# Four value tiles' products cut at 512 and 8, or at 348 and 172, token columns in place of 260 and 260

## The reference

```python
def rmsnorm(x, g):
    y = xf * lax.rsqrt(jnp.mean(xf * xf, axis=-1, keepdims=True) + EPS)
    return (y * g).astype(x.dtype)

def ab_mixer(h, conv_buf, past, w_in, b_f, conv_w, w_out):     # h = rmsnorm(x, g)
    q, k, v, f_lin, b_gate, c_gate, x_in = jnp.split(h @ w_in, AB_SPLITS, axis=-1)
    ...
    logf = jax.nn.log_sigmoid(f_lin + b_f)
    y_a = fox_prompt(q, k, v, logf)            # or fox_decode(...) for the sample tokens
```

## Time and profile before

| what | value |
|---|---|
| time, median of 3 runs | 2090.14 us (2089.59 to 2093.53) |
| the profiled execution's span | 2089.9 us |
| PE busy, share of the span | 2068.6 us, 99% |
| DVE busy | 1125.9 us, 54% |
| ACT busy | 702.9 us, 34% |
| value tiles v0 to v3 on PE | 445.3 to 472.0 us of the span |
| the time of the profiled execution by itself | not given apart; its span lies within the runs' times |

### The profile page before, as it was taken

How to read it: one execution, slowest core, us unless ns; L and a number is a source line. 1 busy time by engine, 2 the same in 40 slices (tenths; PEclk the granted TensorE clock), 3 DMA queues, 4 the chain that set the end, 5 groups by cost and what they waited for, 6 DMA issues and landing times.

```text
span 2089.9 us, 37944 instructions
## 1 busy us (share of the span) xinstructions
PE 2068.6 (99%) x17092; PEld 2046.3 (98%) x17092; DVE 1125.9 (54%) x1509; ACT 702.9 (34%) x877; POOL 47.7 (2%) x95
## 2 busy tenths in 40 slices
PE   8999999999999999999999999999999999999999
PEld 8999999999999999999999999999998999999998
DVE  6443244866768543244686342344898854323467
ACT  5221123423354322122444222122487432212243
POOL 0000000022200000000000000000000000000000
PEclk9999999999999999999999999999999999999999
DMA  5222222145321322222222222222222222222222
GB/s 175 90 90 89 96 102 81 62 153 162 127 108 61 122 81 92 91 102 92 101 82 101 82 96 89 99 84 79 86 97 84 82 101 102 89 94 85 98 92 82
DMA packets 35106, 202.79 MB, mean 97 GB/s; under 512 B 5088, under 2 KB 5376, under 8 KB 17024
## 3 DMA queue, kind: packets, MB, share of 16 engines
q1 hardware_dynamic: 29520, 183.87, 25.0%
q0 software_dynamic: 5424, 16.50, 2.5%
HBM read 193.78 MB, written 4.48 MB: 95 GB/s over the span
## 4 chain that ended last, share of the span: by engine, by line
PE 86%; DVE 11%; ACT 2%; issue 1%; DMA 1%; DVEq 0%; ACTq 0%
PE acc L1825 70%; PE acc L1935 10%; DVE w_lo L1120 2%; DVE t L1233 2%; PE acc L1866 1%; DVE x L1240 1%; DVE act_lo L1246 1%; DMA raw<-in_weights 1%; DVE rs_post L1228 1%; PE acc L2015 1%; PE acc L2069 1%; DVE xsum L1255 1%; DVE rs_pre L1228 0%; PE acc L2093 0%; PE acc L2142 0%
## 5 line engine op out<-in xcount | busy, mean ns | idle before, releaser
L1825 PE MATMUL acc<-act_hi,w_hi 128*128 128x260 f32 x3072 | 621.5, 284 | 0.0
L1825 PE MATMUL acc<-act_hi,w_lo 128*128 128x260 f32 x3072 | 617.8, 283 | 0.0
L1825 PE MATMUL acc<-act_lo,w_hi 128*128 128x260 f32 x3072 | 617.4, 282 | 0.0
L1825 PEld LDWEIGHTS acc<-act_hi,w_hi 128*128 128x128 f32 x3072 | 472.4, 188 | 2.7 <-issue 2.0
L1825 PEld LDWEIGHTS acc<-act_hi,w_lo 128*128 128x128 f32 x3072 | 472.6, 188 | 0.4
L1825 PEld LDWEIGHTS acc<-act_lo,w_hi 128*128 128x128 f32 x3072 | 471.8, 188 | 0.5
L723 ACT ACTIVATE w_hi<-raw 128x2048 fp32r<-128x2048 f32 (+3 forms) x179 | 323.0, 1805 | 297.4 <-DMA raw<-in_weights 297.3
L1120 DVE TENSOR_TENSOR w_lo<-raw,w_hi 128x2048 fp32r<-128x2048 f32 (+3 forms) x179 | 386.4, 2158 | 31.7 <-ACT w_hi L723 31.7
L1370 DVE TENSOR_TENSOR gu<-acc,rs_pre 128x520 f32<-128x520 f32 x164 | 114.3, 698 | 441.1 <-PE acc L1825 441.0
L849 ACT ACTIVATE hid_hi<-gu 128x520 fp32r<-128x520 f32 x86 | 55.0, 639 | 476.6 <-DVE gu L1390 476.6
L1825 PE MATMUL acc<-hid_hi,w_hi 128*128 128x260 f32 x1024 | 206.4, 283 | 0.2
(11 more groups left out here) (308 smaller groups left out, 2141.6 us busy)
## 6 DMA issues: line engine op xcount, KB each, us to landing
raw<-in_weights SPq DMA_DIRECT2D x138, 1024.0 KB, 4.8
raw<-in_weights SPq DMA_DIRECT2D x32, 896.0 KB, 4.5
ring<-in_k_pages POOLq DMA_DIRECT2D x16, 256.0 KB, 3.7
raw<-in_weights SPq DMA_DIRECT2D x12, 256.0 KB, 5.3
x<-in_x SPq DMA_DIRECT2D x8, 260.0 KB, 6.5
out_y<-x SPq DMA_DIRECT2D x8, 260.0 KB, 2.1
ckb<-ch_rows POOLq DMA_DIRECT2D x8, 256.0 KB, 4.5
ring<-in_v_pages POOLq DMA_DIRECT2D x8, 256.0 KB, 3.8
```

What stands on the lines that cost most here:

```text
L1825: ins = nc.tensor.matmul(a[0:width, half, 0:HALF], w[slot][:, at:at + width], m[:, half * HALF:(half + 1) * HALF], start=first and n == 0, ...
```

## The change

The two cuts of a value tile's tokens are no longer equal. For v0 and v1 the first matmul of a pair has 512 columns (a whole bank) and the second 8; for v2 and v3 they have 348 and 172. The number of matmuls and of weight loads stays the same, 48 a tile; so does the order of the pairs. As the two banks no longer hold equal parts, DVE drains a value tile in two instructions, one for each bank, the second behind the first. No other tile is changed.

```diff
+        def value_cut(m):
+            return SEQ if m < 2 else 348
...
                 for m in range(AC):
-                    scaled(v[:, m, :], f"{s}.v{m}")
+                    cut = value_cut(m)
+                    a = acc_of(f"{s}.v{m}")
+                    wait_job(dve, f"{s}.v{m}")
+                    chained(nc.vector.tensor_tensor(v[:, m, 0:cut], a[:, 0, 0:cut], rs_pre[:, 0:cut], ALU.mult))
+                    drains(nc.vector.tensor_tensor(v[:, m, cut:TOK], a[:, 1, 0:TOK - cut], rs_pre[:, cut:TOK], ALU.mult),
+                           f"{s}.v{m}")
                     done(f"{s}.v{m}")
...
-            def chunk(a, slot, at, hi, lo, first, last, width=P):
+            def chunk(a, slot, at, hi, lo, first, last, width=P, cut=HALF):
                 for n, (w, m) in enumerate(((w_hi, hi), (w_hi, lo), (w_lo, hi))):
-                    for half in range(2):
-                        ins = nc.tensor.matmul(a[0:width, half, 0:HALF], w[slot][:, at:at + width],
-                                               m[:, half * HALF:(half + 1) * HALF],
+                    for half, (lo_at, hi_at) in enumerate(((0, cut), (cut, TOK))):
+                        ins = nc.tensor.matmul(a[0:width, half, 0:hi_at - lo_at], w[slot][:, at:at + width],
+                                               m[:, lo_at:hi_at],
...
-                column_tile("v0", "v0", 0)
-                column_tile("v1", "v0", 1, with_keys(0))
-                column_tile("v2", "v2", 0)
-                column_tile("v3", "v2", 1)
+                column_tile("v0", "v0", 0, cut=value_cut(0))
+                column_tile("v1", "v0", 1, with_keys(0), cut=value_cut(1))
+                column_tile("v2", "v2", 0, cut=value_cut(2))
+                column_tile("v3", "v2", 1, cut=value_cut(3))
```

More of the change, by code:

```diff
@@ L1834, in _, with tile @@
             act_in = parts(act_hi, act_lo)
-            def tile(name, n, ks, at, inp, wait=None, width=P, after=None):
+            def tile(name, n, ks, at, inp, wait=None, width=P, after=None, cut=HALF):
                 j = J[name]
@@ L1842, in tile @@
                         wait(c)
-                    ins = chunk(a, n % SLOTS, at(c), *inp(c), c == 0, c == ks - 1, width)
+                    ins = chunk(a, n % SLOTS, at(c), *inp(c), c == 0, c == ks - 1, width, cut)
                     if after is not None:
@@ L2049, in attention, with column_tile @@
                 pair(s, ["k2", "k3"], "k2")
-                def column_tile(name, unit, second, after=None):
+                def column_tile(name, unit, second, after=None, cut=HALF):
                     n = U[f"{s}.{unit}"]
                     wait_unit(n)
-                    tile(f"{s}.{name}", n, KC, lambda c: (2 * c + second) * P, act_in, after=after)
+                    tile(f"{s}.{name}", n, KC, lambda c: (2 * c + second) * P, act_in, after=after, cut=cut)
                 def key_scores(i, r):
```

## The result

The changed kernel took 2101.48 us, the median of three runs (2098.95 to 2102.06), 11.3 us above the median of the kernel before. The ratio worked out from all runs of the two is 1.0045, with a 95% interval of 1.0025 to 1.0065: slower by 9.4 us (5.2 to 13.6).

The account below looks back on a forecast made before the run. PE, busy for 99% of the span, was taken to bound the kernel. Uneven pairs +4.7 and +1.4, drains 0 and a clock fall +1.5 gave +7.6 us on 2089.9: 2097.6 us, range 2094.5 to 2102 (the sum's own bounds 2094.8 to 2100.3).

Parts of the forecast that it names:

- the two-cycle rate of narrow products: Narrow float32r products at two cycles a column: 172 columns take 152 ns; 2099.4 us with a fall of the clock.
- 512 and 8, two tiles: v0 and v1, 48 pairs: a pair takes 338 ns against 239.6, +4.7 us (+4.1 to +5.4).
- 348 and 172, two tiles: v2 and v3, 48 pairs: a pair takes 269 ns, +29.4 ns each, +1.4 us (+0.8 to +2.0).
- drains: Two DVE instructions a value tile add 0.15 to 0.2 us each, hidden from PE: 0, at most 0.2 us uncovered.
- clock in v1 and v2: One fall of the granted clock to 0.50 in v1 or early v2: +1.5 us, bounds 0 and 3.0; chance 0.47.
- rest of the run: Behind the value tiles, PE's later waits for ACT and DVE move along and take nothing back.
- One sign that the prediction named: In the changed profile, the next wide product starts some 113 ns after the narrow one; wide to narrow 222 to 230 ns.
- two sets ahead: Rival: the queue loads two weight sets ahead, hiding both loads of a pair; not slower, 2089.5 us; chance 0.04.
- No fall: Rival: the same sum without the 1.5 us for a fall of the clock, 2096.1 us; chance 0.30.
- A lost rate of narrow products: Rival: narrow float32r products run slower; 2104.5 us at four cycles without a fall, 2099.4 at two with one; chance 0.11.
- Cheaper wide streams: Rival: wide streams cost less than their columns, pairs cheaper by up to 27 ns; 2087 to 2089 us; chance 0.02.
- Later waits absorb the loss: Rival: PE's later waits, 5.4 us, end on work not fed by PE; about 2092 us; chance 0.05.

Follow-up runs that it names:

- the version with v1 spread: Changed kernel with its cuts, but v1's two-column products behind chunks 0, 2, 4 and 6 instead of 3 to 6; 2096.81 us, ratio 1.0027.

## Why the prediction was right, and which term was mis-sized

The direction and the mechanism held, and the time lay inside the range near its upper end. That it lay inside was in part luck: the sum's own bounds end at 2100.3, 1.2 us below the measured time. The range reached on to 2102 to hold the two-cycle rate of narrow products, a rival that the runs refuted. By the steps of the prediction:

| term | predicted us | measured us | read from |
|---|---|---|---|
| 512 and 8, two tiles | +4.7 | +4.6 | v0 8.14 - 5.76, v1 11.81 - 9.59 at full clock |
| 348 and 172, two tiles | +1.4 | +1.5 | v2 and v3 alone, 13.06 - 11.58 |
| drains | 0 | 0 | ratio 1.0002 (0.9993 to 1.0011) |
| clock in v1 and v2 | +1.5 | +4.8 | v1 15.50 - 11.81, v2 7.64 - 6.54, both against the version with v1 spread |
| rest of the run | 0 | -1.1 | +1.6 ahead of v0, -2.7 behind v3 |

**The uneven pairs.** One set of weights waits beside the one in use, as read from the earlier trace rows: the pair pays a bare load. The pair of 512 and 8 was taken as 338 and took 341 to 342; that of 348 and 172 as 269 and took 270 to 272. The parts were off in opposite ways. By the starts of the weight loads in v0 the 512 columns took 230 to 240 ns, not 225, so the surplus grows with the columns (0.434 ns a column in place of 0.417), the alternative that I had set aside; the bare load took 107 to 109 ns, not 113. On the load, the Trainium skill (TensorE: Matmul & The Clock Gate, section LDWEIGHTS (loading the stationary operand)) gives the weights' columns divided by 1.2 in ns, 107 for 128, and the trace agrees at the full clock, with these 107 to 109.

One sign that the prediction named misled. It gave some 113 ns from a narrow product's start to the next wide one's, and well under 100 ns as the sign of two sets ahead. PE's records show 27 ns, and 312 to 321 from a wide product to its narrow one in place of 222 to 230:

```profile
447.48 0.17 PE L1834 MATMUL acc<-act_lo,w_hi 128*128 128x8 f32 x1
447.49 0.30 PEld L1834 LDWEIGHTS acc<-act_hi,w_lo 128*128 128x128 f32 x2
447.51 0.47 PE L1834 MATMUL acc<-act_hi,w_lo 128*128 128x512 f32 x1
```

The load for the wide product began only when the narrow one did (447.49 and 447.48), and the next load followed 108 ns behind it. So I read the 27 ns as a record that starts before the wide product's own weights are in, with the rest of the bare load inside it. The first wide product of v0 bears this out: it follows a product of 260 columns, and its narrow one started 230 ns behind it. The starts of the loads and the 341 ns of a pair decide against two sets ahead; the starts of PE's records could not.

**The clock, the mis-sized term.** I priced a fall as one stretch of 3.41 us, as in the earlier trace rows, where equal pairs followed and the clock came back. Here it lasted 10.24 us, of which 4.8 were lost, more than the 3.0 that I had set as the bound. For v1 the experiments show the two ingredients apart: uneven pairs without dense two-column products kept 1.00 in v2 and v3 and in the spread version of v1; dense two-column products with uneven pairs lost it in two kernels; and twice as many of them with equal pairs lost it as well. Elsewhere no such rule is shown: with equal pairs the clock also fell in c1 with the two-column products spread, and at 523.11 in the kernel before. How long it stays low is argued, not shown: in the changed kernel the clock came back 2.3 us behind the end of v1 (472.89 - 470.55), with uneven cuts in v0 and v1 alone 2.9 us behind it (469.72 - 466.86), and with the two-column products twice at 471.57, again in v2; so the fall's length seems to be set by how early it comes in the alternation. Why it comes earlier in one execution than in another stays open. That I gave a fall 0.47 against 0.30 for none was on the right side: the two kernels with uneven v0 and v1 and dense rounds both had it in their profiled runs.

**The base of the sum.** I added to the profiled span of 2089.9 as though it were that execution's time. In the changed run a span of 2099.8 stands beside a time of 2101.48: 1.7 us lie around the span. So the sum stood too low from the start: by 1.7 us if as much lies around that execution, by 1.0 to 1.2 against the later medians of the kernel before.

**The rivals.** No fall: refuted by the profile; its time, 2096.1, lies near the 2096.81 of the version with v1 spread. A lost rate of narrow products: refuted; at two cycles a column 172 columns would have made the pair some 307 ns, and it took 271. Two sets ahead: refuted, since 512 and 8 would then have cost under 240 ns. Cheaper wide streams: refuted. The Trainium skill's 131 ns a product at 512 columns (the same page, section Back-to-back issue gap) isn't borne out for these products, which take 230 or more by the starts of their loads. Later waits absorb the loss: refuted; the waits of the earlier trace rows stayed at 4.5 and 0.9 us.

## What to carry to other kernels

Where weights change with every product, an uneven split of the moving columns loses as soon as the narrow product is shorter than its neighbour's load. The equal cut hides both loads, and here each column moved to the wide side beyond 300 cost 0.434 ns. In v1 many bare loads close together cost twice, once by themselves and once because the granted clock fell. There it paid to spread the two-column products between wide ones (2096.81 against 2101.48 us); done for all four heads' pages it cost waits and a fall elsewhere (2103.91 us), so make sure that what they claim is free by then. Price a fall of the clock as a range over the whole stretch in which the pattern goes on, and take what lies around the span into the base of the sum.

## What the runs showed of the hardware that was not expected

- At half clock the bare load slows with the streams: 212 ns a two-column product against 112.5, and 640 ns a pair of 512 and 8 against 341.
- The clock can stay at 0.50 for 10.24 and 13.65 us while PE is busy all the time, with loads and products back to back.
- Ahead of the falls in v1 PE's rows look no idler than elsewhere: 28 and 33 products in 3.41 us, PE busy throughout. Busy time alone doesn't foretell them.
- A fall can cost nothing. In eight of the ten profiled executions, the changed kernel's among them, the clock fell for 3.41 us between 1598 and 1617 us, in a stage where PE waits for ACT's `act_hi`. In the changed run the 1.5 us lost came off the wait behind it.
- As I read the records, a wide product's can start before its weights are in: 27 ns behind the narrow product, with 108 ns from its load to the next.
